# Split-fp32 weight rings: one flat array each for the high and the low half, 28672 bytes apart, with new starting places for stationary and moving weights

## The chip, the cores and the metric

One core of a Trainium2 chip runs the whole program. The metric is the device time of one execution in microseconds (us); lower is better. Three executions of the kernel before took 1472.63, 1476.23 and 1477.31 us, with the median at 1476.23 us. A fourth execution was profiled, and all the rows below come from it.

## What is computed

The reference runs two blocks over 256 tokens of width 1024, in fp32. The first block has two layers. Each is an RMS norm, one wide input projection, three mixers side by side (a gated spatial MLP, a latent attention with eight heads, a gated linear recurrence), their three output projections, each under a sigmoid gate, a last projection `w_out`, and a residual sum. The second block has a pooling mixer, a sparse attention, two feed-forward networks of width 2816 with a short convolution, and two gated products. Cut to the first block:

```python
for l in range(DEPTH):                       # 2 layers
    proj = rmsnorm(x, pre_norm_g[l]) @ w_in[l]
    (u, v, z_a, c_q, c_kv, k_rope, z_b, x_c, z_c, g_a, g_b, g_c) = jnp.split(proj, cuts, axis=-1)
    y_a = gmlp_spatial(u, v, ...) * jax.nn.silu(z_a)
    y_b = mla_attention(c_q, c_kv, k_rope, ...) * jax.nn.silu(z_b)
    y_c = rg_lru(x_c, ...) * jax.nn.silu(z_c)
    merged = sum(sigmoid(g_i) * (y_i @ w_proj_i[l]) for i in "abc")
    x = x + rmsnorm(merged @ w_out[l], post_norm_g[l])
```

All weights, some 230 MB, are read from memory once. They are what the change is about.

## The kernel before, in words

**Pieces.** The weights come in 226 slots (`SLOTS`), each of k tiles of 128 rows by n columns, and a slot in two halves, so there are 452 pieces of mostly 128 partitions by 1024 numbers (4096 bytes per partition). Piece 133 is the second half of slot 66. The program walks through them in one order on every engine.

**A piece's way.** SyncE issues its DMA into `raw` (`load`, line 390). ScalarE copies it into `w_hi` as fp32r, a shortened fp32 (`hi`, line 1321). VectorE writes the rest, raw minus high, as `w_lo` (`lo`, line 1877), in the same memory as `raw`. TensorE then makes every product from three matmuls in `three`: high by high (L620), high by low activations or weights (L623), and low by high (L624). Six places of each kind form a ring (`RING`), piece p has place p modulo 6.

**Stationary and moving.** In `features` and `queries` the weights are the stationary operand, 128 columns at a time, and the activations move, 256 columns. In `tokens` and `tokens_in_turn` the activations are stationary and 512 weight columns move (256 in a few slots). Slots of 8 or 3 tiles are the stationary kind, those of 2 or 4 tiles the moving kind. `place` and `weights` put pieces of the first kind 64 bytes further on than those of the second; both kinds keep the same address modulo 128 in all six places, but since the places are 4160 bytes apart, not modulo 256 or 512. Counted from `h_hi`, and modulo 512, the high half of a moving piece starts at 0, 128, 128, 256, 256, 384 in the places 0 to 5, its low half at 384, 0, 0, 128, 128, 256. A stationary piece starts at 64, 64, 192, 192, 320, 320 (high) and 448, 448, 64, 64, 192, 192 (low).

**Order and waits.** Each engine runs its queue strictly in the order of the program. SyncE waits for `w_begun` at line 389 before it overwrites a place: TensorE raises this count by one with the first L620 of each piece, so that count p - 4 says that piece p - 5 has begun and piece p - 6 is finished. In `tokens_in_turn`, the form of the last projection of a stage, four pieces are run through for the first 128 tokens and then again for the other 128; the second to the fourth of them raise the count only in the second pass. ScalarE waits for the landing (`raw_full`), VectorE for ScalarE (`hi_done`), TensorE for VectorE (`w_split`). ScalarE and VectorE take the pieces two slots ahead (`ahead=2`), at fixed points between their other work: for the last projection of a layer, ScalarE casts the two pieces of slot 66 (132 and 133) and only then squares the sums of the two groups of tokens (L1339) and takes their root (L1367), on which VectorE's residual sum (L2353), the next layer's norm (L1897) and TensorE's transposes (L745) depend.

**Memory.** Per partition `par` (3584 bytes of parameters) comes first, then small arrays, `x`, `h_hi`, `h_lo`, `m` of 8192 bytes each, six `w_hi` of 4160 bytes, six `raw`/`w_lo` of 4160, `hf`, and the overlay that holds all the other activations (`c_hi`, `ya_hi`, `yb_hi`, `yc_hi`, `y2_hi`, ...).

Of the kernel before, what the change touches and what calls it, by code (L numbers as in the profile page):

```python
# [8 lines left out]
F32 = mybir.dt.float32  # L9
F32R = mybir.dt.float32r  # L10
# [6 lines left out]
P = 128  # L17
# [9 lines left out]
QKD = NOPE + ROPE  # L27
# [16 lines left out]
PIECE = 1024  # L44
RING = 6
SHIFT = 16
# [40 lines left out]
def weight_slots():  # L87

    out = []
    for l in range(L):  # L90
        out += [(8, 256)] * 10 + [(8, 256), (8, 128), (8, 256), (8, 64)] + [(3, 2 * QKD)] * 4 + [(2, 1024)] * 2
        out += [(8, 256)] * 4 + [(4, 512)] * 4 + [(8, 256)] * 8 + [(4, 512)] * 20
        out += ([(2, 512)] + [(4, 512)] * 2) * 2 + [(4, 512)] * 4
    out += [(2, D), (8, 256)]
    for l in range(L):
        out += [(8, 256)] * FT + ([(2, 512)] + [(4, 512)] * 5) * 2 + [(4, 512)] * 4
        if l == 0:
            out += [(8, 256)] * 6 + [(8, 48)] + [(8, 256)] * 4 + [(2, D)] * 5
    return out


SLOTS = STEPS = weight_slots()
# [1 line left out]
DOWN = [(0, 2)] + [(2 + 4 * n, 4) for n in range(5)]  # L104


def landed(piece):

    return 16 * sum(2 if SLOTS[p // 2] == (3, 2 * QKD) else 1 for p in range(piece % RING, piece + 1, RING))


def place(slot):

    k, n = SLOTS[slot]
    return SHIFT if k in (3, 8) else 0


def halves(k):

    return (0, (k + 1) // 2), ((k + 1) // 2, k)  # L120


CONST = {}
# [111 lines left out]
def program(nc, slots, ins, out):  # L235
    ctx = ExitStack()
    with ctx:
        def sb(name, shape, dt=F32):
            return ctx.enter_context(nc.sbuf_tensor(name, shape, dt))

        def overlay(*plans):

            made = {}
            for number, plan in enumerate(plans):
                with ExitStack() as scope:
                    for name, shape, dt in plan:
                        t = scope.enter_context(nc.sbuf_tensor(name or f"pad{number}_{len(made)}", shape, dt))
                        made[name or f"pad{number}_{len(made)}"] = t
            return made
# [3 lines left out]


        cst = sb("cst", [P, NCONST])
        par = sb("par", [P, 7 * P])
        st = sb("st", [P, 12])
        cell = sb("cell", [P, 1])
        sink = sb("sink", [P, 8])
# [5 lines left out]
        h_hi = sb("h_hi", [P, KT, TOK], F32R)  # L265
        h_lo = sb("h_lo", [P, KT, TOK], F32R)
        m = sb("m", [P, KT, TOK])
        w_hi = [sb(f"w_hi{b}", [P, PIECE + SHIFT], F32R) for b in range(RING)]
        landing = overlay([(f"raw{b}", [P, PIECE + SHIFT], F32) for b in range(RING)])
        raw = [landing[f"raw{b}"] for b in range(RING)]  # L270
        w_lo = [sb(f"w_lo{b}", [P, PIECE + SHIFT], F32R) for b in range(RING)]
        hf = sb("hf", [P, 2, TOK])

        o = overlay(
# [87 lines left out]
        def piece_of(slot, half):  # L362

            piece = 2 * slot + half
            k0, k1 = halves(SLOTS[slot][0])[half]
            return piece, piece % RING, (k1 - k0) * SLOTS[slot][1]

        def weights(t, slot, b, size=PIECE):

            first = place(slot) if b % 2 == 0 else SHIFT - place(slot)  # L370
            return t[b][:, first:first + size]

        block = ctx.enter_context(nc.Block())
        attn_scale = 1.0 / math.sqrt(QKD)
# [3 lines left out]
        def _(sp):  # L378
            w = Walk(sp, "sp")

            def load(j, src):

                slot = w.n["S"] + j
                k, n = SLOTS[slot]
                assert list(src.shape) == [P, k, n], (slot, src.shape, k, n)
                for half, (k0, k1) in enumerate(halves(k)):
                    piece, b, size = piece_of(slot, half)
                    if piece >= RING:
                        sp.wait_ge(sems["w_begun"], piece - RING + 2)
                    sp.dma_start(weights(raw, slot, b, size).rearrange("p (k n) -> p k n", n=n), src[:, k0:k1, :])\  # L390
                        .then_inc(sems[f"raw_full{b}"], 16)

            def load_query(j, src):

                for half, (c0, c1) in enumerate(((0, NOPE), (NOPE, QKD))):
                    piece, b, size = piece_of(w.n["S"] + j, half)
                    sp.wait_ge(sems["w_begun"], piece - RING + 2)
                    to = weights(raw, w.n["S"] + j, b, size).rearrange("p (k h n) -> p k h n", k=3, h=2)
                    for h in range(2):
                        sp.dma_start(to[:, :, h, :], src[:, :, h * QKD + c0:h * QKD + c1])\  # L400
                            .then_inc(sems[f"raw_full{b}"], 16)
# [4 lines left out]
            first = CONST["ones"][0]  # L406
# [198 lines left out]
        def _(pe):  # L605
            w = Walk(pe, "pe")

            def half_ready(slot, half):

                piece, b, _ = piece_of(slot, half)  # L610
                pe.wait_ge(sems["w_split"], piece + 1)
                return b
# [17 lines left out]
            def features(j, job, cols, act, k0=0, start=True, stop=True, ready=None, tiles=KT,  # L630
                         only=(0, 1), last_use=True, width=P):

                slot = w.n["S"] + j
                k_tiles, n = SLOTS[slot]
                hi, lo = act
                banks = [w.bank("J", job + t) for t in range(len(cols))]
                if start:
                    for t, bank in enumerate(banks):
                        pe.wait_ge(free[bank], w.turn("J", job + t))
                parts = [(half, k, ka) for half, (ka, kb) in enumerate(halves(k_tiles)) if half in only  # L640
                         for k in range(ka, kb)]
                for half, k, ka in parts:
                    if k == ka:
                        b = half_ready(slot, half)
                    if ready:
                        pe.wait_ge(sems[ready], w.value(ready, k0 + k + 1 - tiles))
                    for t, col in enumerate(cols):
                        mm = three(ps[banks[t]][0:width, 0:TOK], col(weights(w_hi, slot, b), k - ka, n), col(weights(w_lo, slot, b), k - ka, n),
                                   hi[:, k0 + k, :], lo[:, k0 + k, :],
                                   start and k == parts[0][1], stop and k == parts[-1][1],  # L650
                                   last_use and k == ka and t == 0)
                        if k == parts[-1][1] and stop:
                            mm.then_inc(sems[f"full{banks[t]}"], 1)
# [658 lines left out]
        def _(act):  # L1312
            w = Walk(act, "act")

            def hi(j, half, ahead=2):

                slot = w.n["S"] + j + ahead
                if slot < len(SLOTS):
                    piece, b, size = piece_of(slot, half)
                    act.wait_ge(sems[f"raw_full{b}"], landed(piece))  # L1320
                    act.copy(weights(w_hi, slot, b, size), weights(raw, slot, b, size)).then_inc(sems["hi_done"], 1)  # L1321
# [1468 lines left out]
```

## Time and profile before

| | |
|---|---|
| median of three runs | 1476.23 us (1472.63 to 1477.31) |
| the profiled execution | 1472.04 us, its span 1470.3 us |
| mean granted TensorE clock | 0.994 of full speed |
| busy | TensorE 1423.9 us (97%), its weight loads 1283.6 us, VectorE 1051.4, ScalarE 870.0 |
| chain that ended last | TensorE 78%, VectorE 12%, ScalarE 5%, DMA 2%, issue 2% |

The span runs from the first to the last instruction; the execution's own time has 1.7 us more around it. Matmuls overlap in the pipeline, so what one costs is not the length that its row gives but the distance from its start to the start of the next one. TensorE is nearly always busy, yet the chain leaves it for 22% of the span: there it is VectorE, ScalarE or a landing that sets when TensorE can go on.

### The profile page before, as it was taken

The page shows a single profiled execution, that of the slowest core. Times are in us where ns is not written, and L with a number is a line of the kernel's source. Part 1 is how long each engine was busy: PE and PEld are TensorE (multiplying, and loading weights), DVE is VectorE, ACT ScalarE, POOL GpSimd, SP SyncE. Part 2 cuts the span into 40 slices and gives each one's busy share as a digit, 9 for nine tenths or more (in the row PEclk, how much of TensorE's full clock was granted, in tenths as well). Part 3 has the DMA queues.
Part 4 walks back from the last instruction along what each step waited for, and adds up shares of the span by engine and source line. Part 5 has one row for each costly group of instructions (what it writes and reads, how often), then busy time and mean ns, then how long its engine had stood idle before and what let it go on. Part 6 is the DMA issues. An engine that isn't in the chain of part 4 may idle for free.

```text
span 1470.3 us, 23062 instructions
## 1 busy us (share of the span) xinstructions
PE 1423.9 (97%) x9283; PEld 1283.6 (87%) x9283; DVE 1051.4 (72%) x1601; ACT 870.0 (59%) x1522; POOL 85.2 (6%) x138
## 2 busy tenths in 40 slices
PE   8999999999999999999999989999989989999997
PEld 8988999788789989897888789998889878999886
DVE  7736669886676447699985778885676655888756
ACT  7465756564465656575545656664683553766546
POOL 9100000006000000000000000000000000000000
PEclk9999999999999999999999999999999999999999
DMA  8615476566656344665675437666545103666553
GB/s 256 190 49 151 123 235 188 174 191 190 197 144 183 83 122 144 186 188 171 192 223 199 156 120 223 211 204 191 158 145 145 45 1 97 209 196 192 188 179 115
DMA packets 189210, 240.98 MB, mean 164 GB/s; under 512 B 19086, under 2 KB 133954, under 8 KB 189104
## 3 DMA queue, kind: packets, MB, share of 16 engines
q1 hardware_dynamic: 183232, 228.66, 51.3%
q0 software_dynamic: 5776, 10.82, 2.3%
q8 instruction: 74, 1.21, 0.3%
q14 instruction: 32, 0.26, 0.1%
q10 hardware_dynamic: 96, 0.03, 0.0%
HBM read 238.42 MB, written 1.05 MB: 163 GB/s over the span
## 4 chain that ended last, share of the span: by engine, by line
PE 78%; DVE 12%; ACT 5%; DMA 2%; issue 2%; DVEq 0%; SPq 0%
PE bank L620 23%; PE bank L623 23%; PE bank L624 23%; DVE w_lo L1877 4%; PE bank L837 2%; PE bank L1216 2%; ACT w_hi L1321 1%; DVE rec L2001 1%; ACT T L1818 1%; DMA raw<-in_w_out 1%; DMA raw<-in_mla_w_ukv 1%; DMA raw<-in_w_in 1%; PE bank L1202 1%; PE bank L1130 1%; ACT S L1514 1%
## 5 line engine op out<-in xcount | busy, mean ns | idle before, releaser
L1877 DVE TENSOR_TENSOR w_lo<-raw,w_hi 128x1024 fp32r<-128x1024 f32 (+2 forms) x452 | 519.3, 1170 | 214.6 <-ACT w_hi L1321 211.7
L1321 ACT CAST w_hi<-raw 128x1024 fp32r<-128x1024 f32 (+2 forms) x452 | 448.0, 1009 | 278.6 <-DMA raw<-in_w_in 112.9
L620 PE MATMUL bank<-h_hi,w_hi 128*128 128x256 f32 (+1 forms) x1640 | 457.9, 279 | 6.6 <-DVE h_lo L1913 4.2
L623 PE MATMUL bank<-h_lo,w_hi 128*128 128x256 f32 (+1 forms) x1640 | 455.4, 278 | 0.0
L624 PE MATMUL bank<-h_hi,w_lo 128*128 128x256 f32 (+1 forms) x1640 | 455.1, 277 | 0.0
L620 PEld LDWEIGHTS bank<-h_hi,w_hi 128*128 128x128 f32 (+1 forms) x1640 | 308.0, 188 | 9.6 <-issue 7.8
L623 PEld LDWEIGHTS bank<-h_lo,w_hi 128*128 128x128 f32 (+1 forms) x1640 | 308.2, 188 | 0.1
L624 PEld LDWEIGHTS bank<-h_hi,w_lo 128*128 128x128 f32 (+1 forms) x1640 | 308.0, 188 | 0.0
L620 PE MATMUL bank<-w_hi,h_hi 128*128 128x512 f32 (+1 forms) x464 | 178.7, 385 | 2.7 <-DVE h_lo L1913 1.7
L623 PE MATMUL bank<-w_lo,h_hi 128*128 128x512 f32 (+1 forms) x464 | 176.9, 381 | 0.0
L624 PE MATMUL bank<-w_hi,h_lo 128*128 128x512 f32 (+1 forms) x464 | 176.8, 381 | 0.0
L620 PEld LDWEIGHTS bank<-w_hi,h_hi 128*128 128x128 f32 x464 | 87.2, 188 | 21.3 <-issue 4.0
L624 PEld LDWEIGHTS bank<-w_hi,h_lo 128*128 128x128 f32 x464 | 87.2, 188 | 18.3
L623 PEld LDWEIGHTS bank<-w_lo,h_hi 128*128 128x128 f32 x464 | 87.4, 188 | 17.0
L620 PE MATMUL bank<-w_hi,y_hi 128*128 128x512 f32 x176 | 69.5, 395 | 0.0
L623 PE MATMUL bank<-w_lo,y_hi 128*128 128x512 f32 x176 | 69.1, 392 | 0.0
L624 PE MATMUL bank<-w_hi,y_lo 128*128 128x512 f32 x176 | 69.0, 392 | 0.0
L2424 DVE SCALAR_TENSOR_TENSOR ug<-bank,par,ug 128x255 f32<-128x255 f32 x88 | 40.4, 480 | 22.9 <-ACT ug L1334 21.3
L1334 ACT ACTIVATE ug<-bank,par 128x256 f32<-128x256 f32 x44 | 22.5, 561 | 51.6 <-PE bank L624 51.6
L837 PE MATMUL bank<-xc,wg 128*128 128x256 f32 x208 | 45.8, 381 | 1.2 <-ACT R L1482 1.2
L837 PEld LDWEIGHTS bank<-xc,wg 128*128 128x128 f32 x208 | 39.3, 190 | 7.3 <-ACT R L1482 2.0
L2424 DVE SCALAR_TENSOR_TENSOR ua<-bank,par,ua 128x255 f32<-128x255 f32 x88 | 40.3, 479 | 5.3 <-ACT ua L1334 3.7
(366 smaller groups left out, 2086.3 us busy)
## 6 DMA issues: line engine op xcount, KB each, us to landing
raw<-in_w_in SPq DMA_DIRECT2D x160, 512.0 KB, 3.8
raw<-in_ffn_up SPq DMA_DIRECT2D x88, 512.0 KB, 3.7
raw<-in_ffn_down SPq DMA_DIRECT2D x40, 512.0 KB, 4.4
raw<-in_w_proj_a SPq DMA_DIRECT2D x16, 512.0 KB, 3.5
raw<-in_w_proj_b SPq DMA_DIRECT2D x16, 512.0 KB, 3.5
raw<-in_w_proj_c SPq DMA_DIRECT2D x16, 512.0 KB, 3.6
raw<-in_w_out SPq DMA_DIRECT2D x16, 512.0 KB, 3.6
raw<-in_ple_gate SPq DMA_DIRECT2D x16, 512.0 KB, 4.5
```

Source lines behind the costliest of these rows:

```text
L620: first = pe.matmul(out_, lh, rh, start=start, stop=False)
L623: pe.matmul(out_, lh, rl, start=False, stop=False)
L624: return pe.matmul(out_, ll, rh, start=False, stop=stop)
L837: mm = pe.matmul(acc(b), wg[:, g, rep, pair, :], xc[:, 5 * rep + i_, :], start=(n == 0), stop=(n == len(near) - 1))
L1130: mm = pe.matmul(ps[b][:, 75 * n:75 * n + 75].rearrange("p (g n) -> p g n", g=NG + 1), w1[:, n, k, :], cc[:, 4 * n:4 * n + 5, 2 * k:2 * k ...
L1202: mm = pe.transpose(ps[b][:, n * P:(n + 1) * P], src, c["ident"])
L1216: mm = pe.matmul(o_, pt, vsw[:, k, a, g * HD:(g + 1) * HD], start=k == 0, stop=k == qt)
L1321: act.copy(weights(w_hi, slot, b, size), weights(raw, slot, b, size)).then_inc(sems["hi_done"], 1)
L1334: act.activation(dst, acc(b), func, bias=bias, scale=scale)\
L1514: ins_ = act.activation(S[:, hd, :], S[:, hd, :], ACT.Exp, bias=sm[:, 1, col + hd:col + hd + 1], accum_out=sm[:, 2, col + hd:col + hd + 1])
L1877: dve.tensor_tensor(weights(w_lo, slot, b, size), weights(raw, slot, b, size), weights(w_hi, slot, b, size).bitcast(F32), ALU.subtract).th ...
L2424: ins_ = dve.scalar_tensor_tensor(u_[:, n, d:TOK], ps[b][:, 0:TOK - d], col(i * 2 + (conv_row(l, 2 - d) + c0 + n)), u_[:, n, d:TOK], ALU.m ...
```

## The change

The twelve arrays of the rings become two flat ones, `w_hi` and `w_lo`, with places exactly 4096 bytes apart, and `par` moves in between them, so that `w_lo` begins 28672 bytes (7 times 4096) behind `w_hi`. Moving pieces start at the beginning of their place. Stationary ones start 192 bytes in (high) and 64 bytes in (low, and `raw`). Since a full stationary piece then reaches past its place's end, a new planner, `ring_places`, works out the place of each piece (`WHERE`), and the last older piece whose bytes it meets (`BEHIND`); SyncE waits for that piece to be finished.

```diff
+def place(slot, high=False):
+    k, n = SLOTS[slot]
+    return (3 * SHIFT if high else SHIFT) if k in (3, 8) else 0
+def ring_places():
+    where, behind = [], []
+    def extents(piece, b):
+        k0, k1 = halves(SLOTS[piece // 2][0])[piece % 2]
+        size = (k1 - k0) * SLOTS[piece // 2][1]
+        return [(b * PIECE + at, b * PIECE + at + size) for at in (place(piece // 2), place(piece // 2, high=True))]
+    def meet(one, other):
+        return any(f < e2 and f2 < e for (f, e), (f2, e2) in zip(one, other))
+    for piece in range(2 * len(SLOTS)):
+        b = (where[-1] + 1) % RING if where else 0
+        if where and meet(extents(piece, b), extents(piece - 1, where[-1])):
+            b = (b + 1) % RING
+        older = [p for p, at in enumerate(where) if meet(extents(piece, b), extents(p, at))]
+        where.append(b)
+        behind.append(older[-1] if older else None)
+    return where, behind
...
-        par = sb("par", [P, 7 * P])
...
-        w_hi = [sb(f"w_hi{b}", [P, PIECE + SHIFT], F32R) for b in range(RING)]
-        landing = overlay([(f"raw{b}", [P, PIECE + SHIFT], F32) for b in range(RING)])
-        raw = [landing[f"raw{b}"] for b in range(RING)]
-        w_lo = [sb(f"w_lo{b}", [P, PIECE + SHIFT], F32R) for b in range(RING)]
+        w_hi = sb("w_hi", [P, RING * PIECE + P], F32R)
+        par = sb("par", [P, 7 * P])
+        raw = overlay([("raw", [P, RING * PIECE + SHIFT], F32)])["raw"]
+        w_lo = sb("w_lo", [P, RING * PIECE + 2 * SHIFT], F32R)
...
-            first = place(slot) if b % 2 == 0 else SHIFT - place(slot)
-            return t[b][:, first:first + size]
+            first = b * PIECE + place(slot, high=t is w_hi)
+            return t[:, first:first + size]
...
-                    if piece >= RING:
-                        sp.wait_ge(sems["w_begun"], piece - RING + 2)
+                    if BEHIND[piece] is not None:
+                        sp.wait_ge(sems["w_begun"], BEHIND[piece] + 2)
...
-                    sp.wait_ge(sems["w_begun"], piece - RING + 2)
+                    sp.wait_ge(sems["w_begun"], BEHIND[piece] + 2)
```

Worked out by the planner's own rule over the 452 pieces: no place is ever skipped, so piece p keeps place p modulo 6. `BEHIND` is p - 6 for 415 pieces, none for the first six, and p - 5 for 31: 42 to 44, 56 to 58, 60, 132 to 136, 174 to 176, 188 to 190, 192, 266 to 268, 270, 344 to 346, 348, 376 and 378 to 380. They are the first stationary pieces after moving ones, whose overhang meets the beginning of the next place, where a moving piece still lies.

## Rows read from the trace of the kernel before

**Rows 1.** The page: bandwidth in 40 slices, transfers (issue, count, KB, median us to landing).
```profile
GB/s 256 190 49 151 123 235 188 174 191 190 197 144 183 83 122 144 186 188 171 192 223 199 156 120 223 211 204 191 158 145 145 45 1 97 209 196 192 188 179 115
...
raw<-in_w_in SPq DMA_DIRECT2D x160, 512.0 KB, 3.8
```

**Rows 2.** Groups of instructions, forms apart: L620 with 512 moving weight columns, largest and smallest.
```profile
L620 PE MATMUL bank<-w_hi,h_hi 128*128 128x512 f32 x416 | 164.9, 396 | 1.0 <-issue 1.0
...
L620 PE MATMUL bank<-w_hi,p_hi 128*128 128x512 f32 x16 | 6.3, 393 | 0.0
```

**Rows 3.** Timeline of TensorE, a moving stretch: first L620 of six pieces (start us, us).
```profile
303.13 0.39 PE L620 MATMUL bank<-w_hi,h_hi 128*128 128x512 f32 x1
...
305.90 0.39 PE L620 MATMUL bank<-w_hi,h_hi 128*128 128x512 f32 x1
...
311.39 0.40 PE L620 MATMUL bank<-w_hi,h_hi 128*128 128x512 f32 x1
...
316.98 0.39 PE L620 MATMUL bank<-w_hi,h_hi 128*128 128x512 f32 x1
...
319.75 0.39 PE L620 MATMUL bank<-w_hi,yb_hi 128*128 128x512 f32 x1
```

**Rows 4.** Timeline of TensorE, a stationary stretch: first L620 of two pieces, six pieces apart.
```profile
890.28 0.28 PE L620 MATMUL bank<-h_hi,w_hi 128*128 128x256 f32 x1
...
906.60 0.28 PE L620 MATMUL bank<-h_hi,w_hi 128*128 128x256 f32 x1
```

**Rows 5.** Timeline of SyncE's queue: issues of pieces 133, 134 and 346.
```profile
406.49 0.37 SPq L390 DMA_DIRECT2D raw<-in_w_in  x1
...
413.42 0.37 SPq L390 DMA_DIRECT2D raw<-in_w_in  x1
...
1064.30 0.37 SPq L390 DMA_DIRECT2D raw<-in_w_kv  x1
```

**Rows 6.** Timeline of ScalarE at the first layer's end.
```profile
410.18 1.05 ACT L1321 CAST w_hi<-raw 128x1024 fp32r<-128x1024 f32 x1 [1.64 <-DMA raw<-in_w_in]
411.81 0.60 ACT L1339 ACTIVATE G<-bank 128x512 f32<-128x512 f32 x1 [0.58 <-PE bank L624]
...
415.53 0.30 ACT L1367 ACTIVATE st<-st 128x1 f32<-128x1 f32 x1
417.33 0.60 ACT L1339 ACTIVATE G<-bank 128x512 f32<-128x512 f32 x1 [1.51 <-PE bank L624]
```

**Rows 7.** Chain of waits there: the last matmul before it and the next layer's first.
```profile
417.07 0.24 PE bank L624
...
424.06 0.43 PE bank L620
```

**Rows 8.** Timeline of ScalarE at the second block's gate.
```profile
1062.12 1.05 ACT L1321 CAST w_hi<-raw 128x1024 fp32r<-128x1024 f32 x1 [1.61 <-DMA raw<-in_w_kv]
...
1066.47 0.63 ACT L1339 ACTIVATE G<-x 128x512 f32<-128x512 f32 x1 [1.48 <-DVE x L2477]
...
1068.24 0.69 ACT L1326 ACTIVATE G<-bank,st 128x512 f32<-128x512 f32 x1 [1.05 <-PE bank L624]
```

**Rows 9.** Chain of waits through the gMLP stages of both layers.
```profile
198.02 4.29 DMA raw<-in_w_in
...
202.33 1.05 ACT w_hi L1321
...
204.55 2.29 DVE ln L2186
...
618.85 4.20 DMA raw<-in_w_in
```

**Rows 10.** Waits of the weight loads from 185 to 330 us (total, times, longest).
```profile
PEld bank L932 <- DVE hf L2242: 2.2, 4, 0.7
```

**Rows 11.** Windows: busy us and count of each engine, granted clock, DMA.
```profile
200.00:300.00 100.00, 98.54 (x638) 88.49 (x637) 92.56 (x137) 61.46 (x83) 0.54 (x1) 1.00 0.63 185
424.00:428.00 4.00, 3.94 (x20) 3.97 (x21) 3.57 (x8) 4.00 (x9) 0.00 (x0) 0.57 0.50 137
```

More of the change, by code:

```diff
@@ L104, with landed @@
 DOWN = [(0, 2)] + [(2 + 4 * n, 4) for n in range(5)]
-def landed(piece):
-    return 16 * sum(2 if SLOTS[p // 2] == (3, 2 * QKD) else 1 for p in range(piece % RING, piece + 1, RING))
-def place(slot):
+def place(slot, high=False):
     k, n = SLOTS[slot]
-    return SHIFT if k in (3, 8) else 0
+    return (3 * SHIFT if high else SHIFT) if k in (3, 8) else 0
 def halves(k):
     return (0, (k + 1) // 2), ((k + 1) // 2, k)
+def ring_places():
[14 more added lines that the diff above has]
+    return where, behind
+WHERE, BEHIND = ring_places()
+def landed(piece):
+    return 16 * sum(2 if SLOTS[p // 2] == (3, 2 * QKD) else 1 for p in range(piece + 1) if WHERE[p] == WHERE[piece])
 CONST = {}
@@ L365, in piece_of @@
             k0, k1 = halves(SLOTS[slot][0])[half]
-            return piece, piece % RING, (k1 - k0) * SLOTS[slot][1]
+            return piece, WHERE[piece], (k1 - k0) * SLOTS[slot][1]
         def weights(t, slot, b, size=PIECE):
-            first = place(slot) if b % 2 == 0 else SHIFT - place(slot)
-            return t[b][:, first:first + size]
+            first = b * PIECE + place(slot, high=t is w_hi)
+            return t[:, first:first + size]
         block = ctx.enter_context(nc.Block())
```

## The prediction

> **What bounds the kernel now.** I read the page first: TensorE is busy 97% of the span, at nearly full clock. So two things count: how close its matmuls follow each other, and the few places where it stands. The groups of instructions, forms apart, tell how many matmuls read their moving operand from the rings: seven groups of L620 with 512 columns, 416 instructions in the largest and 16 in the smallest, 832 in all [rows 2], each with its L623 and L624. That is 2496 matmuls, or 208 full pieces of 12. The rest of the pieces are the stationary operand.
>
> The timeline of TensorE gives the price of a piece. Moving: from 303.13 to 305.90 in place 0 (2.77 us), 5.49 us for the two in places 1 and 2 (2.745 each), 5.59 for places 3 and 4 (2.795 each), 2.77 in place 5; the mean is 16.62 / 6 = 2.77 us, or 231 ns a matmul [rows 3]. The pairs of equal places modulo 512 cost the same, so the differences follow the place, and a place differs from the next in its address modulo 512 alone. At one column per cycle of 2.4 GHz a matmul would take 213 ns, a piece 2.56 us. (This is an estimate; a stationary piece's 256 columns in 113 ns allow it.) So some 18 ns a matmul, 0.21 us a piece, is there to be had. Stationary: six pieces in a row take 16.32 us, 2.72 each, 24 matmuls of 113.3 ns, whatever the place [rows 4].
>
> Last I read the chain of waits and the queues where TensorE stands. At the first layer's end it goes from the last matmul at 417.07 to the next layer's first at 424.06, over ScalarE and VectorE [rows 7]. In the gMLP stage it goes from a landing at 198.02 + 4.29 over ScalarE's cast to VectorE [rows 9], which then works almost without a pause up to the wait named next (93% busy in that hundred, TensorE 99%) and for which TensorE's L932 waits four times [rows 10, 11].
>
> **The change, part by part.**
>
> *Stationary places (192 and 64 bytes).* The new pair is, modulo 512 and against `h_hi`, just the pair that places 2 and 3 have today. The six pieces of [rows 4] run through all six places and leave no room for a difference between them, so I take 0 for the stationary pieces; bounds 0 to +0.01 us for each of some 200 pieces, since a row is read to 0.01.
>
> *Moving places, equal for high and low.* This combination is nowhere in the trace: high at 0 exists (place 0, 2.77 us), low at 0 exists (places 1 and 2, 2.745), both together don't. Half of the triples (416 of 832, [rows 2]) run against `h_hi`. The others run against arrays behind the rings, and those shift: they lay 49920 bytes behind `w_hi` and will lie 53376 behind it, 3456 more, which is 128 modulo 256, so for them the new meeting is 128. The two nearest values are 2.77 and 2.745, and I take today's mean of 2.77, thus 0. Bounds inside the trace: 2.745 and 2.795, thus -5 and +5 us over 208 pieces. Beyond the trace the gain ends at 208 x 0.21 = -44 us.
>
> The Trainium skill, "SBUF — State Buffer", section "Who interferes with whom", gives TensorE two independent read ports and says that PE never waits on anyone; by this alone no address would matter and the term would be 0. The rows, with 2.745 against 2.795 us, show that addresses do matter a little here, so the rule is not the whole of it, and my bounds stay open on both sides.
>
> *ScalarE and VectorE.* They read and write as many numbers as before, and their casts and subtractions come at the same points of their queues. 0.
>
> *The planner's waits.* This is the part that the words of the change don't name. For 31 pieces SyncE waits for p - 5 in place of p - 6 to be finished. The count asked for (p - 3) is exactly the one that the next piece asks for now, so each of the 31 is issued when its successor is issued now. Most of them have microseconds to spare in front of TensorE, and nothing urgent behind their cast. Four of the 31 are not so.
>
> 1. Piece 133. It is issued at 406.49 now and will be at 413.42, when 134 is [rows 5], for piece 129 raises the count only in the second pass of the last projection. From issue to cast it takes 410.18 - 406.49 = 3.69 us [rows 5, 6], so the cast starts at 417.1 and not at 410.18. Queued behind it on ScalarE are the squares of the first 128 tokens (now at 411.81), their root, the squares for the next norm and the root after them (415.53, 0.30 long), and then the squares of the second 128 tokens, which TensorE released for 417.33 [rows 6]. From the cast's end (410.18 + 1.05 = 411.2) to the end of that root (415.8) the work takes 4.6 us. After the change: 417.1 + 1.05 + 4.6 = 422.8, where the second squares now start at 417.33. So the next layer begins 5.4 us later. Who waits: VectorE's residual sum, the norm, the transposes, and TensorE, whose cover until 417.07 is used up. Bounds: +4.9 (if VectorE's own subtraction of 133 is not in the way) and +6.3 (if the whole delay of the squares shows).
> 2. Piece 345, the same at the second block's gate. It will be issued at 1064.30, when 346 is [rows 5]. With the 3.8 us to landing that the page has for the largest group [rows 1] its cast starts at 1068.1 in place of 1062.12. From the cast's end to the end of the squares of 1066.47 is 4.0 us now [rows 8], so the last gate's activation starts at 1068.1 + 1.05 + 4.0 = 1073.2 in place of 1068.24: +4.9 us. Bounds +4 to +6.
> 3. Piece 58, issued ahead of 59 now, joins it at 198.02, and both then share the DMA engines. 59 is the landing of the chain [rows 9]. A transfer of 0.52 MB takes 2.0 us at the 256 GB/s of the fullest slice [rows 1]; part of it overlaps, so I take +1.4. Behind it are ScalarE's cast of 202.33, the evacuation of v, and VectorE's L2186 at 204.55, from where VectorE is full up to the product for which L932 waits [rows 9, 10]. Bounds 0 and +2.
> 4. Piece 192 joins 193 at 618.85 [rows 9] in the second layer: +1.4 again, same bounds.
>
> Pieces 42 and 43 (and 174, 175) also delay a cast, by 5 us, but TensorE has its attention scores to make there; I take 0, upper bound +1 each. The longer stand at the two layer ends can move the clock's fall: in today's first stretch after it the granted clock is 0.57 [rows 11], between the levels of 1.2 and 2.4 GHz. I take 0; upper bound +2 each.
>
> **Sum.** 5.4 + 4.9 + 1.4 + 1.4 = +13.1 us, against the profiled execution's 1472.04: 1485. That execution lies 4 us below the median of the three runs, so for the median I say 1476.2 + 13.1 = 1489. What a measurement of this kernel can tell from no change is about 0.3%, 4.4 us.
>
> **The rivals.**
>
> *A. Equal places free the moving matmuls (faster).* One mechanism: high and low moving rows that follow each other at the same address modulo 4096 no longer meet the weight load half-way. For it: the pieces differ with the place, and 0.21 us lies open in each. Stationary pieces have activations of this sort moving (`h_lo` is 8192 behind `h_hi`) and are even. Against it: L624 and the next L620 move high rows at equal addresses already today, in every piece, and the pieces still cost 2.745 us at least [rows 3]. Stationary pieces are even at every distance of their two halves [rows 4]. Half of 0.21 on 208 pieces gives -22 us, all of it -44: with the waits' 13 the time is 1467 or 1445. It decides from 64 ns a piece (13.1 / 208) on; for over 0.3% faster, 84 ns. Chance 0.27.
>
> *B. The later issues are hidden (no change).* If the landing of 133 and 345 came earlier than 3.7 us after the issue, or ScalarE's order there left room, only the 2.8 us of the gMLP stages or less stay: 1476 to 1479. Against it: the order of the queue is in the rows, and the count is raised at a fixed matmul. Chance 0.10.
>
> *C. The moving pieces get worse, on top of the waits.* At 2.795 us for each, +5: 1494; with a wait's clock cost 1498. Chance 0.13.
>
> *D. The change does nothing to the addresses that matter*, since half of the activations shift with it: that is my forecast, the waits alone. Chance 0.50.
>
> **How the numbers follow.** The forecast with its own bounds (waits 9 to 17, moving -5 to +5) is 1480 to 1498. A reaches down to 1445, of which I leave out the lower part; so 1457 to 1499. Slower by over 0.3%: D and C, less the cases where a part of A's gain eats the waits, 0.59. Within 0.3%: B and such cases, 0.14. Faster: 0.27.
>
> **What would show it.** The issue of 133 at the time of 134's, its cast right before the squares, and TensorE's stand at the layer's end of 12 us in place of 7; the same at the gate; VectorE's L2186 1.4 us later against the stage's start. Six moving pieces in 16.5 to 16.8 us, all six alike; stationary ones at 2.72. I am wrong if a moving piece takes 2.70 or less, if stationary pieces leave 2.72, or if the two stands don't grow.

## The result and the profile after

The changed kernel takes **1497.89 us** (median of four runs, 1484.98 to 1501.65), the kernel before 1476.77 in its four runs beside it. The ratio is 1.0127, with a 95% interval from 1.0097 to 1.0158: slower by 1.3%. The forecast of 1489 had the sign and 13 of the 21 us.

The profiled execution took 1501.65 us with a span of 1499.9, 29.6 more than the span of before. So the traces have more to explain (29.6 us) than the medians (21). The page of the changed kernel, busy time and the granted clock in 40 slices, with the median landing of the largest group of transfers:

```profile
PE 1446.1 (96%) x9283; PEld 1305.4 (87%) x9283; DVE 1052.9 (70%) x1601; ACT 870.9 (58%) x1522; POOL 85.6 (6%) x138
...
PEclk9999999999999999999999999999989979999999
...
GB/s 252 186 46 134 142 224 190 176 187 198 177 139 179 78 124 137 211 183 173 192 225 182 147 148 216 216 185 184 140 116 157 29 1 98 210 184 184 185 180 113
...
raw<-in_w_in SPq DMA_DIRECT2D x160, 512.0 KB, 3.8
```

TensorE works as many matmuls as before and is busy 22 us longer; its idle time grew by only 7. Part of the 22 is the same work at a lower granted clock, as the windows below show. The median landing of the largest group is what it was [rows 1].

**Moving pieces.** Groups of instructions, forms apart, beside [rows 2], and the timeline of TensorE at the first L644 (L620 before) of five pieces, beside [rows 3]:

```profile
L644 PE MATMUL bank<-w_hi,h_hi 128*128 128x512 f32 x416 | 163.0, 392 | 1.1 <-issue 1.1
```

```profile
310.16 0.39 PE L644 MATMUL bank<-w_hi,h_hi 128*128 128x512 f32 x1
...
312.88 0.39 PE L644 MATMUL bank<-w_hi,h_hi 128*128 128x512 f32 x1
...
321.04 0.39 PE L644 MATMUL bank<-w_hi,h_hi 128*128 128x512 f32 x1
...
323.77 0.40 PE L644 MATMUL bank<-w_hi,yb_hi 128*128 128x512 f32 x1
...
326.56 0.39 PE L644 MATMUL bank<-w_hi,yb_hi 128*128 128x512 f32 x1
```

A piece out of `h` takes 2.72 us in every place (310.16 to 312.88; three pieces from 312.88 to 321.04), where it took 2.745 to 2.795. A piece out of `yb` takes 2.79 (323.77 to 326.56). Before, the pieces out of the arrays other than `h` took 2.77 in the mean over the six places, as those out of `h` did.

**Stationary pieces.** The timeline of TensorE, first L644 of pieces 134 and 135, and of 278 and 279; 134 and 278 both lie in place 2 (beside [rows 4]):

```profile
439.15 0.28 PE L644 MATMUL bank<-h_hi,w_hi 128*128 128x256 f32 x1
...
441.87 0.28 PE L644 MATMUL bank<-h_hi,w_hi 128*128 128x256 f32 x1
...
897.60 0.28 PE L644 MATMUL bank<-h_hi,w_hi 128*128 128x256 f32 x1
...
900.45 0.28 PE L644 MATMUL bank<-h_hi,w_hi 128*128 128x256 f32 x1
```

The same place, the same weights' addresses, the same `h`: 2.72 us the first time, 2.85 the second. From 869.4 us, and again from 1281.0, 351 triples in a row go at the slower pace.

**The first layer's end.** ScalarE's timeline, beside [rows 6], and the chain of waits, beside [rows 7]:

```profile
420.96 1.04 ACT L1345 CAST w_hi<-raw 128x1024 fp32r<-128x1024 f32 x1 [6.00 <-DMA raw<-in_w_in]
421.91 0.59 ACT L1363 ACTIVATE G<-bank 128x512 f32<-128x512 f32 x1
...
426.43 0.58 ACT L1363 ACTIVATE G<-bank 128x512 f32<-128x512 f32 x1
```

```profile
417.01 3.92 DMA raw<-in_w_in
420.96 1.05 ACT w_hi L1345
422.04 1.23 DVE w_lo L1901
...
433.63 0.36 PE bank L644
```

The chain now runs through the transfer of piece 133, which is issued at 417.01 (beside [rows 5]), and through its cast. From the start of piece 131 (419.31 us) to that of 132 (433.63) it is 14.31 us, where it was 8.30. At the gate, beside [rows 8]:

```profile
1080.13 1.05 ACT L1345 CAST w_hi<-raw 128x1024 fp32r<-128x1024 f32 x1 [5.14 <-DMA raw<-in_w_kv]
...
1084.46 0.63 ACT L1363 ACTIVATE G<-x 128x512 f32<-128x512 f32 x1 [1.48 <-DVE x L2501]
...
1085.09 0.67 ACT L1350 ACTIVATE G<-bank,st 128x512 f32<-128x512 f32 x1
```

Piece 343 to piece 344 takes 13.70 us, where it took 7.68. In the gMLP stage the waits of the weight loads (total us, times, longest) show a new one beside that of [rows 10]:

```profile
PEld bank L956 <- DVE hf L2266: 2.4, 4, 0.7
PEld bank L644 <- DVE uz L2245: 1.1, 1, 1.1
```

The clock: windows (busy us of the five engines, granted clock, DMA share, GB/s) over the stand at the first layer's end, beside [rows 11], and over the sparse attention, of the changed kernel first and then of the kernel before:

```profile
424.00:428.00 4.00, 0.61 (x3) 0.64 (x4) 2.98 (x8) 2.46 (x8) 0.00 (x0) 0.51 0.01 5
...
1177.20:1248.50 71.30, 68.03 (x438) 60.37 (x436) 37.93 (x65) 30.38 (x93) 0.00 (x0) 0.86 0.03 10
```

```profile
1159.20:1224.50 65.30, 60.34 (x438) 54.00 (x437) 37.92 (x65) 30.45 (x93) 0.00 (x0) 0.97 0.03 11
```

The lower clock falls elsewhere now. Before, the first stand (415.76 to 424.06) ran at 1.00 and piece 132 behind it at 0.62. Now the lower clock lies inside the stand and is over before piece 132. The window of piece 132 before, then those of the stand and of piece 132 now:

```profile
424.06:428.50 4.44, 4.44 (x24) 4.44 (x25) 4.01 (x9) 4.44 (x9) 0.00 (x0) 0.62 0.45 124
```

```profile
419.31:433.63 14.32, 6.92 (x40) 6.15 (x38) 8.55 (x21) 7.29 (x21) 0.00 (x0) 0.76 0.30 95
433.63:436.43 2.80, 2.80 (x25) 2.80 (x25) 2.59 (x7) 2.80 (x8) 0.00 (x0) 1.00 0.41 94
```

So of the 6.0 us by which the first stand grew, piece 132 gives 1.6 back (4.44 us, now 2.80).

**Where the 29.6 us are.** Stationary triples (L644, L647, L648) out of `h`, those without a pause among them and outside the sparse attention's pieces (358 to 365): a mean of 350.9 ns for 340.8, times 1522, is +15.4 us. The two stands: +6.0 each. The gMLP stages: +1.2 and +0.5. Moving triples: 392 out of `h` at 681.1 ns for 692.9, -4.6; some 400 out of the other arrays at about 698 for 693, +2.1. The sparse attention, at the half clock for longer, +6.1. The first piece after the gate, at the half clock too, +1.9. That is 34.6. Pieces 132, 163, 164, 268 and 349 gave back 6.5 between them (0.7 to 1.7 each). Behind 163 and 349 TensorE waited 2.3 and 1.5 us, now 0.6 and 0.3. Pieces 132, 164 and 268 ran at 0.62, 0.72 and 0.65 of the clock before and run at 1.00 now. The rest, 1.5, is spread.

### The profile page after: what moved, and what is told of

It is laid out like the page before. It is cut to its first block, busy times and chain, and to the rows that moved or that the text cites. A ratio compares the mean times of both kernels' runs of the same rounds, so it can differ in the third digit from the quotient of the medians.

```text
span 1499.9 us, 23062 instructions
## 1 busy us (share of the span) xinstructions
PE 1446.1 (96%) x9283; PEld 1305.4 (87%) x9283; DVE 1052.9 (70%) x1601; ACT 870.9 (58%) x1522; POOL 85.6 (6%) x138
## 4 chain that ended last, share of the span: by engine, by line
PE 79%; DVE 11%; ACT 4%; DMA 4%; issue 2%; SPq 0%; DVEq 0%
PE bank L644 23%; PE bank L647 23%; PE bank L648 23%; DVE w_lo L1901 4%; PE bank L861 2%; PE bank L1240 2%; DMA raw<-in_w_in 2%; DVE rec L2025 1%; ACT w_hi L1345 1%; ACT T L1842 1%; PE bank L798 1%; DMA raw<-in_w_out 1%; DMA raw<-in_mla_w_ukv 1%; PE bank L769 1%; PE bank L1226 1%
## 5 line engine op out<-in xcount | busy, mean ns | idle before, releaser
L644 PE MATMUL bank<-h_hi,w_hi 128*128 128x256 f32 (+1 forms) x1640 | 459.1, 280 | 6.3 <-DVE h_lo L1937 3.9
L647 PE MATMUL bank<-h_lo,w_hi 128*128 128x256 f32 (+1 forms) x1640 | 460.6, 281 | 0.0
L648 PE MATMUL bank<-h_hi,w_lo 128*128 128x256 f32 (+1 forms) x1640 | 456.2, 278 | 0.0
L644 PEld LDWEIGHTS bank<-h_hi,w_hi 128*128 128x128 f32 (+1 forms) x1640 | 307.4, 187 | 9.3 <-issue 6.2
L648 PEld LDWEIGHTS bank<-h_hi,w_lo 128*128 128x128 f32 (+1 forms) x1640 | 307.1, 187 | 0.0
L647 PEld LDWEIGHTS bank<-h_lo,w_hi 128*128 128x128 f32 (+1 forms) x1640 | 306.7, 187 | 0.1
L644 PE MATMUL bank<-w_hi,h_hi 128*128 128x512 f32 (+1 forms) x464 | 176.8, 381 | 2.7 <-DVE h_lo L1937 1.6
L647 PE MATMUL bank<-w_lo,h_hi 128*128 128x512 f32 (+1 forms) x464 | 175.5, 378 | 0.0
L648 PE MATMUL bank<-w_hi,h_lo 128*128 128x512 f32 (+1 forms) x464 | 175.5, 378 | 0.0
L644 PEld LDWEIGHTS bank<-w_hi,h_hi 128*128 128x128 f32 x464 | 87.1, 188 | 19.9 <-issue 4.0
L648 PEld LDWEIGHTS bank<-w_hi,h_lo 128*128 128x128 f32 x464 | 87.1, 188 | 16.5
L647 PEld LDWEIGHTS bank<-w_lo,h_hi 128*128 128x128 f32 x464 | 87.1, 188 | 16.0
L644 PE MATMUL bank<-w_hi,y_hi 128*128 128x512 f32 x176 | 69.7, 396 | 0.0
L648 PE MATMUL bank<-w_hi,y_lo 128*128 128x512 f32 x176 | 69.5, 395 | 0.0
L647 PE MATMUL bank<-w_lo,y_hi 128*128 128x512 f32 x176 | 69.5, 395 | 0.0
```

Source lines behind the costliest of these rows:

```text
L644: first = pe.matmul(out_, lh, rh, start=start, stop=False)
L647: pe.matmul(out_, lh, rl, start=False, stop=False)
L648: return pe.matmul(out_, ll, rh, start=False, stop=stop)
```

## The experiments

Each theory was written down before its run. Times are medians; a ratio is to the kernel before on the same chip. Stands are from the start of piece 131 to that of 132, and from 343 to 344.

### The waits alone

The kernel before, only with the later issues of the changed one:

```diff
-                        sp.wait_ge(sems["w_begun"], piece - RING + 2)
+                        sp.wait_ge(sems["w_begun"], piece - RING + 2 + (piece in LATER))
```

`LATER` holds all 31 pieces in the first run and 133 and 345 in the second.

> The layout of before; only SyncE's wait is one piece later for the 31 pieces that the planner names (count p - 3 in place of p - 4). By my theory the waits cost what I summed: the next layer's first matmul and the one after the second block's gate each 5 to 6 us later, the two gMLP stages about 1.4 and 1.4: 13 us, ratio 1.009. Rival (the waits are hidden, the slower kernel comes from the addresses alone): ratio 1.000 to 1.003. In both, stationary pieces stay at 2.72 us and moving ones at 2.745 to 2.795.

> As waits_all, but the later wait for pieces 133 and 345 alone. Theory: 10 to 12 us of the 13, ratio 1.007 to 1.008, by two stands of TensorE that each grow by 5 to 6 us. Rival (the 31 waits cost a little everywhere, in the DMA queue): a fifth of waits_all at most.

All 31: 1488.87 us, ratio 1.0086 (1.0048 to 1.0125), thus 11.0 us more. The two alone: 1485.79, ratio 1.0054 (1.0030 to 1.0078), 7.9 more. TensorE with the two alone, first matmul of pieces 131, 132, 343 and 344 (L623 here is what L620 was before):

```profile
418.48 0.39 PE L623 MATMUL bank<-w_hi,h_hi 128*128 128x512 f32 x1
...
432.80 0.36 PE L623 MATMUL bank<-h_hi,w_hi 128*128 128x256 f32 x1 [0.85 <-DVE h_lo L1916]
...
1072.00 0.39 PE L623 MATMUL bank<-w_hi,h_hi 128*128 128x512 f32 x1
...
1085.79 0.35 PE L623 MATMUL bank<-h_hi,w_hi 128*128 128x256 f32 x1 [0.54 <-DVE h_lo L1916]
```

The stands are 14.3 and 13.8 us, as in the changed kernel, and the pieces stay at 2.72 and 2.77. So two of the 31 waits make both stands, and the waits are about half of the loss. The two stands are 12.1 us longer in the trace and cost 7.9 in the medians; the interval (4.4 to 11.5 us) stops just short of it. But piece 132 gives 1.6 back here too (2.83 us), so that 10.5 are left in the trace, and these lie within the interval.

### The places of the stationary weights

First the kernel before with nothing but the parameters moved, so that places 2 and 3 get exactly the addresses of the changed kernel for `h`, high and low:

```diff
-        par = sb("par", [P, 7 * P])
...
         w_hi = [sb(f"w_hi{b}", [P, PIECE + SHIFT], F32R) for b in range(RING)]
+        par = sb("par", [P, 7 * P])
```

> The kernel of before with one line moved: par stands between the w_hi and the w_lo arrays. Counted from h_hi modulo 4096 nothing changes for the high halves, the low ones come 3584 bytes later; modulo 512 nothing changes at all. A stationary piece has (high, low) = (64, -64) in places 0 and 1, (192, 64) in 2 and 3, which is the pair of the changed kernel, and (320, 192) in 4 and 5. Theory (the pair high 192, low 64 against the moving activations, exactly, costs 2.853 us a piece): places 2 and 3 take 2.85, the others 2.72; some 50 pieces x 0.133, 7 us slower, ratio 1.004. Rival 1 (the absolute addresses of the h arrays, moved down by 3584, or high and low rings 128 less than a multiple of 4096 apart): all six places 2.85, 20 us slower, ratio 1.013. Rival 2 (equal places in a flat array): all 2.72, ratio 1.000.

1478.27 us, ratio 1.0005 (0.9980 to 1.0029). The stationary pieces took 2.720 us in all places, but for pieces 2, 3, 44 and 45, in places 2 and 3, which took 2.85. Most pieces in these two places were fast, so the theory that the addresses cost 2.853 whenever they are met fell. What it left out stood in the trace of before all the time, at the first L620 of pieces 45 (place 3) and 46:

```profile
164.12 0.28 PE L620 MATMUL bank<-h_hi,w_hi 128*128 128x256 f32 x1
...
166.98 0.28 PE L620 MATMUL bank<-h_hi,w_hi 128*128 128x256 f32 x1
```

2.86 us. In the trace of before 76 of 1513 stationary triples are slow (351 to 361 ns in place of 340), 63 of them in four runs of 14 to 17 in places 2 and 3, and each run ends where place 4 begins. So there are **two paces**. The slow one begins where the row of stationary triples has been interrupted, by a pause (ahead of piece 8 one step takes 250 ns in place of 113, ahead of piece 350 TensorE waits 1.5 us) or by other matmuls (those of L774 ahead of 44 and 176). It holds while the pieces keep such addresses, and not all pairs of places hold it for long. Inside an uninterrupted row the pace in this trace changes 15 times, always from slow to fast. Not every interruption leads to a long slow stretch. In the changed kernel all six places have the pair of places 2 and 3, which holds it. The places in it were then changed, everything else kept (waits too):

```diff
-    return (3 * SHIFT if high else SHIFT) if k in (3, 8) else 0
+    return (SHIFT if high else 7 * SHIFT) if k in (3, 8) else 0
```

and with `SHIFT` for both, and with `3 * SHIFT` (high) and `7 * SHIFT` (low). Where the low half moves to 448, the arrays are made longer too, so that what lies behind them keeps its address modulo 1024.

> The changed kernel with stationary weights 64 bytes (high) and 448 bytes (low) into their place, which modulo 512 is the pair of places 0 and 1 before; the low ring's array is 1024 bytes longer, so that what lies behind keeps its address modulo 1024. Waits as in the changed kernel. Theory (the pair of starting places): stationary pieces fed by h back to 2.72 us, moving ones as in the changed kernel, so 20 us less than the changed kernel's 1498: 1478 to 1482, ratio to before 1.000 to 1.004. Rival (flat rings 28672 apart, or the moved h arrays): stationary pieces stay at 2.85, ratio 1.013.

> The changed kernel, with the high halves of the stationary weights 64 bytes into their place in the place of 192; the low ones stay at 64, everything else stays (waits too). In the changed kernel a stationary piece took 2.853 us in two thirds of its groups and 2.720 in the others; with 64/448 (high/low) it took 2.720 in nearly all. Theory H, the 192 of the high half is what lets the slower pitch last: 2.720 us, and the run is as the one of 64/448, 1488 to 1490 us. Theory L, the low half at 64 is what does it: 2.853 in most, and 1496 to 1500 us. If it needs both, then it is fast as in H, and the run with 192/448 is fast too. The moving pieces stay (2.72 out of h, 2.79 out of y).

> The changed kernel, with the low halves of the stationary weights 448 bytes into their place in the place of 64; the high ones stay at 192. Theory H, the 192 of the high half does it: 2.853 us in most stationary pieces and 1496 to 1500 us. Theory L, the 64 of the low half does it: 2.720, and 1488 to 1490 us. If it needs the pair (192, 64), it is fast here and in the run with 64/64.

| bytes into the place (high, low) | time, us | ratio (interval) | slow among the triples |
|---|---|---|---|
| 192, 64 (the change) | 1497.89 | 1.0127 (1.0097 to 1.0158) | 999 of 1522 |
| 64, 448 | 1488.51 | 1.0062 (1.0040 to 1.0085) | 23 of 1509 |
| 64, 64 | 1491.94 | 1.0108 (1.0072 to 1.0145) | 459 of 1529 |
| 192, 448 | 1507.30 | 1.0207 (1.0168 to 1.0247) | 1495 of 1525 |

The timeline of TensorE, pieces 278 and 279, with 192/448 and then with 64/448:

```profile
906.75 0.28 PE L644 MATMUL bank<-h_hi,w_hi 128*128 128x256 f32 x1
...
909.57 0.28 PE L644 MATMUL bank<-h_hi,w_hi 128*128 128x256 f32 x1
```

```profile
896.70 0.28 PE L644 MATMUL bank<-h_hi,w_hi 128*128 128x256 f32 x1
...
899.42 0.28 PE L644 MATMUL bank<-h_hi,w_hi 128*128 128x256 f32 x1
```

2.82 against 2.72 us. Each count of triples comes from one profiled execution, without pieces 358 to 365. Among these the run with 64/448 had 28 slow ones, in pieces 362 to 365, behind other matmuls: this pair can hold the slow pace as well, but rarely did. Neither theory (the high half's 192 alone, or the low half's 64 alone) holds: 192 for the high half is slow with either low place (66% and 98% of the triples in the two traces), 64 is fast with one and in two thirds with the other. The high place matters more, the low one shifts the share. With 64/448 the change loses 10.6 us in place of 21. The 1478 to 1482 that were expected left the waits out: what is left is about what they cost alone (11.0).

### The places of the moving pieces

The kernel with 64/448, its overlay with `y`, `ya`, `yb` and `yc` 128 bytes lower, so that they begin equal to the weights modulo 1024, as `h` does:

```diff
-        w_lo = sb("w_lo", [P, RING * PIECE + 2 * SHIFT + 2 * P], F32R)
+        w_lo = sb("w_lo", [P, RING * PIECE + 2 * P], F32R)
```

> The kernel with 64/448, and the overlay behind the rings (y, ya, yb, yc and the rest) 128 bytes lower, so that the arrays y of the moving pieces begin on the same 512 as the weights, as h does already. Theory, a moving piece is fastest where its weights and its stationary side lie alike: the pieces out of y, ya, yb and yc fall from 2.79 to 2.72 us as those out of h did, some 110 pieces by 0.07 is 7 to 8 us, so 1480 to 1482 against 1488.5. Rival, the 2.72 of h is of h's own place or of its reader and not of the difference: y pieces stay at 2.79 or so, 1487 to 1490 us. The two stands before pieces 132 and 344 stay at 13.5 to 14.5 us in both.

1485.15 us, ratio 1.0064 (1.0044 to 1.0084). Pieces 96 and 97, out of `yb`:

```profile
321.59 0.39 PE L644 MATMUL bank<-w_hi,yb_hi 128*128 128x512 f32 x1
...
324.31 0.39 PE L644 MATMUL bank<-w_hi,yb_hi 128*128 128x512 f32 x1
```

2.72 us, as forecast: at equal places a moving piece takes 2.72 us, whatever it is multiplied with. All 416 such triples gain 17 ns, 7 us in all. The medians show 3.4 of them, and the ratios (1.0062 and 1.0064) none, so a gain in time isn't shown by this run; the clock is taken up below.

Then no shift anywhere, in the same kernel, so that no piece reaches into the next place and no issue is later:

```diff
-    return (SHIFT if high else 7 * SHIFT) if k in (3, 8) else 0
+    return 0
```

> The kernel y_aligned with no shift in any place: high and low weights, moving and stationary, all begin their place, so that no piece reaches into the next place and the planner finds no later issue (all 446 wait as in the kernel before). The two stands are 8.3 and 7.7 us, moving pieces 2.72. What the stationary pieces take at places equal to h tells the rule: if equal places are as good for them as for moving ones, 2.72 us and 1467 to 1470 us in all, faster than before. If a stationary matmul needs its weights apart from the moving operand, 2.80 us or more a piece, some 150 to 206 pieces, and 1480 us or more.

1491.88 us, ratio 1.0102 (1.0071 to 1.0133). Pieces 278 and 279:

```profile
896.48 0.28 PE L644 MATMUL bank<-h_hi,w_hi 128*128 128x256 f32 x1
...
899.36 0.28 PE L644 MATMUL bank<-h_hi,w_hi 128*128 128x256 f32 x1
```

2.88 us, in 1528 of 1540 triples. Where weights move, equal places are the best; where they are stationary, they are the worst that was tried. The stands are back at 8.3 and 7.7 us, which shows again that only the reach into the next place makes them.

### The stands taken away

In the first layer's last product and in the second block's gate, the cast and the subtraction of 133 and 345 go behind the squares and additions in their queues. ScalarE's part at the product; VectorE's and the gate's are alike:

```diff
-                    hi(0, 0), hi(0, 1)
+                    hi(0, 0)
+                    if (l, n) != (0, 1):
+                        hi(0, 1)
...
                             square_part(1, t)
+                    if (l, n) == (0, 1):
+                        hi(0, 1)
```

It was first made in both layers, on the kernel with aligned `y`; then in the first alone; then so on the changed kernel itself, and on the kernel before.

> The kernel before it (y_aligned), and in the last product of the first layer and in its gate the cast and the subtraction of the last of the pieces there (133 and 345, whose transfer the change lets start one piece later) moved behind the squares, the square roots and the additions of x in the queues of the scalar and the vector engine, which no longer wait for that transfer. Theory, the 13 us of the later issues are these two stands: they fall from 14 us to 8 or less, 10 to 12 us less than y_aligned, and with the 2.72 of the moving pieces 1468 to 1472 us, below the kernel before (1477.9). Rival, the transfers are late anyway and the stand is only taken at piece 133 itself: 14 us turns into 8 with 5 more at the next piece, and the time stays at 1480.

> The kernel aligned_moved, with the cast and the subtraction of the second layer's last product back where the kernel before has them: there the move made TensorE stand 13.95 us before piece 264 in the place of 5.5 (the piece is needed in that same product, and no transfer was late for it). The rest stays. Theory, this stand is the whole of what aligned_moved lost to its forecast: 5.5 us before piece 264, 8.5 and 7.7 before 132 and 344, and 1477.3 less 8.4 is 1469 us (1467 to 1471), below the kernel before. Rival, the 8.4 us come back as a stand in the second layer's feed-forward part, since piece 268 starts a wait of its own: 1474 to 1478 us.

> The changed kernel itself (places 192/64) with the same two moves of the cast and subtraction of pieces 133 and 345 in the first layer. Theory, waits and places are separate terms of its loss: the two stands fall back to 8 us, 10 to 12 us less than the changed kernel's 1497.9, and 1486 to 1488 us are left, of which some 9 are the slow stationary pieces less the faster moving ones. The stationary pieces stay at 2.853 in most groups. Rival, which groups are slow hangs on when TensorE starts after a wait: then their number moves with the stands and the time comes out anywhere from 1478 to 1492.

> The control for aligned_moved_once: the kernel before, its rings, places and waits untouched, with the same move of the cast and subtraction of pieces 133 and 345 behind the squares and additions. Theory, the move only takes a late transfer off the path, and in the kernel before these transfers are 5 us earlier, so that there is nothing to take off: stands of 8.3 and 7.7 us as they are, 1477 us within 2, and the 8 us that aligned_moved_once gained are the moving pieces at equal places. Rival, the move is itself worth something (the cast and subtraction, 2.3 us, lie ahead of the squares): stands of 6 to 7 us and 1472 to 1474 us.

In both layers: 1477.28 us, ratio 1.0004 (0.9984 to 1.0025), with stands of 8.5 and 7.7 us, and a new one in the second layer's last product, where the moved piece is needed at once. The waits of TensorE there (total us, times, longest):

```profile
PE bank L644 <- DVE w_lo L1904: 6.6, 1, 6.6
```

In the first layer alone: **1469.55 us, ratio 0.9953 (0.9933 to 0.9974)**, faster than the kernel before by 7.9 us, where 1469 was expected. The first matmul of pieces 131, 132, 343 and 344:

```profile
416.89 0.39 PE L644 MATMUL bank<-w_hi,h_hi 128*128 128x512 f32 x1
...
425.26 0.55 PE L644 MATMUL bank<-h_hi,w_hi 128*128 128x256 f32 x1 [0.73 <-DVE h_lo L1942]
...
1068.07 0.39 PE L644 MATMUL bank<-w_hi,h_hi 128*128 128x512 f32 x1
...
1075.80 0.36 PE L644 MATMUL bank<-h_hi,w_hi 128*128 128x256 f32 x1 [0.92 <-DVE h_lo L1942]
```

8.4 and 7.7 us, as before the change, though piece 133 is issued as late as in the changed kernel (414.60 us, 2.3 ahead of the start of piece 131, as 417.01 was there).

On the changed kernel: 1491.44 us, ratio 1.0105 (1.0073 to 1.0136), 6.5 less than the change; 10 to 12 were expected. The stands are gone (8.4 and 7.7 us). In its profiled execution 557 of 1519 stationary triples were slow, not 999, and the time lies where the rival put it. One trace of each kernel can't tell, though, whether the stands change which groups are slow or whether that varies between executions anyway. That execution took 1487.5 us and was the fastest of the four; what the triples did in the other three isn't seen.

On the kernel before: 1474.33 us, ratio 0.9987 (0.9966 to 1.0008), stands of 8.4 and 7.75 us. The interval holds no change; it leaves room for a gain of up to 5 us, of which the stands show nothing. So the 7.9 us are mainly the moving pieces: 392 triples by 12 ns and some 400 by about 12, 9.6 us, less 1.7 and 1.4 us at the two gMLP stages.

## Why the prediction came out as it did

- **Stationary places, "I take 0", bounds 0 to +0.01 us a piece: this step failed.** The prediction had named stationary pieces that leave 2.72 as a sign of being wrong. The term cost +15.4 us in the profiled execution, and putting the weights elsewhere gave 9.4 us back in the medians. The step read six pieces in one stretch that ran at the fast pace [rows 4] and took this for "whatever the place". It saw rightly that the new pair is the one of places 2 and 3. But it asked of them only in a stretch where places 0, 1, 4 and 5 end the slow pace or it wasn't taken up, while places 2 and 3 took 2.86 us a few hundred microseconds earlier. A bound of 0.01 us from one stretch was no bound.
- **The waits, +13.1 us: right, within their bounds.** Their forecast was +5.4 and +4.9 at the two stands; the trace has +6.0 and +6.0, and the runs with nothing but the waits cost 11.0. Against the start of piece 131 the second squares moved from +1.57 us (417.33) to +7.12 (426.43), 5.55 later, and the last gate's activation, against piece 343, by 4.7. The order in the queue was read rightly; the rest fits TensorE's transposes: eight of them take 1.94 us at a granted clock of 0.50 (427.39), where they took 1.04 at 1.00 (417.13). What piece 132 gives back, 1.6 us, the prediction didn't see.
- **The gMLP stages, +1.4 each: near it.** +1.2 and +0.5 in this pair of traces, at the steps from piece 61 to 62 and from 193 to 194. Over all fourteen profiles these steps take 3.1 us in the mean in the five kernels whose issues of 58 and 192 aren't later, and 4.2 in the nine others: +1.1 each. VectorE's L2186 (now L2210, at 208.3 us) is 1.2 later against piece 56. The wait is a new one, L644 for `uz`, and L932's stays as it was.
- **Pieces 42, 43, 174 and 175, 0 with an upper bound of +1 each: a little low.** The steps from piece 39 to 40 and from 171 to 172 take 11.1 us in those five kernels and 11.5 to 12.0 in the nine others, so the later issues cost some 0.5 us in each layer.
- **The moving pieces, 0 within -5 and +5: right by its bound, by chance in its value.** Half gained 4.6 us and half lost 2.1. Rival A was right in kind for the half out of `h`, and wrong in size: 0.05 us a piece and not 0.1 to 0.2. Its limit of 213 ns a matmul was met by no run; the fastest is 2.72 / 12 = 227 ns. The test "16.5 to 16.8 us for six" failed for those out of `h` (16.32), and held for the others (6 x 2.79 = 16.74).
- **The clock, 0: not settled.** With the longer stands the mean granted clock was 0.983 to 0.986 in all ten runs of the kernel with aligned `y`, and 0.986 to 0.996 in the ten where only the stands were taken away. Those two differ by 15.6 us, the stands in the traces by 12. That the clock makes the other 3.6 isn't shown. A good part of the lower mean is counted inside the stands themselves: in the changed kernel 14.3 us at 0.76 and 13.7 at 0.77 are worth 0.0044 of the whole span's mean (an estimate from these windows), and there TensorE mostly waits. And one +6 is no effect of the change: the sparse attention, 65.3 us in the profile of before, took 70.2 in the run with only the parameters moved, with a granted clock of 0.90:

```profile
1160.40:1230.60 70.20, 65.24 (x438) 58.69 (x437) 37.91 (x65) 30.44 (x93) 0.00 (x0) 0.90 0.03 10
```

  Over the fourteen profiles it takes 63.7 to 65.3 us four times and 70.2 to 71.6 ten times, with long stands and with short ones in either group. It makes up 6.1 of the 8.5 us by which the two traces differ more than the medians do.

- **The sum.** 1489 was 9 us low: the stationary term. The forecast was right in its sign because the waits alone are enough for it. That 1497.9 still lies within 1457 to 1499 is luck: the upper end stood for waits of 17 us and moving pieces at +5, and neither came. (In rival A, 13.1 / 208 is 63 ns and not 64, which changes nothing.)

Addresses do matter to TensorE here. By the Trainium skill, "SBUF — State Buffer", section "Who interferes with whom", PE has two independent SBUF read ports and shares neither with another engine. The runs show that this isn't the whole of it: with the same instructions a stationary piece took 2.72 us with 64/448 and 2.88 with 0/0. Whether the ports have a part in it no run shows.

**Still open.** What starts a long slow stretch and what ends it (which wait, which neighbour) isn't known; it was seen only that such stretches begin behind an interruption, and end at another one or at places that don't hold them. Why 64/64 is slow in a third of the triples isn't either. With pairs that allow both paces the time should spread more from run to run (the changed kernel's four lie 16.7 us apart), but four runs are too few to show it: 27 of the kernel before lie 14.0 apart.

## What to carry to other kernels

Price an address by the longest stretch of the trace that uses it and by its worst one, not by one steady stretch: count all triples by place before saying "whatever the place". In triples like these (fp32r, 512 or 256 moving columns), equal offsets of weights and activations were the best where the weights are the moving side, and the worst of those tried where they are the stationary side. Where a change makes a transfer later, move the work that waits for it behind what is urgent in that queue, after looking up, in each layer, when the piece is needed.

## What the hardware showed that was not expected

- The same stationary matmuls at the same addresses run at two paces, 340 or 353 to 360 ns for three, and the changed kernel keeps the slow one for as many as 351 triples.
- Moving matmuls of 512 columns follow each other at 227 ns at equal places, at 229 to 233 at others; stationary triples take 340 ns at 64/448 and 360 at equal places.
- Inside an uninterrupted row of stationary triples the pace of before changed 15 times, each time from slow to fast.
- A longer stand can cost less than its length: with the first one at 14.3 us the half clock fell inside it, and piece 132 behind it took 2.80 us in place of 4.44.
- Kernels with two stands of 14 us had a mean granted clock of 0.984 to 0.987 over their runs (seven kernels), those with stands of 8 us 0.989 to 0.993; single runs overlap.
- The sparse attention takes either 63.7 to 65.3 us or 70.2 to 71.6, whatever the kernel (fourteen profiles).
